# A decoder step on one core: the forget step on VectorE split, its subtraction six slots later; the memory's sums of squares three slots later

## The chip, the cores and the metric

The kernel runs on one core of one Trainium2 chip. The core's engines are TensorE (PE in the rows; its weight loads are PEld), VectorE (DVE), ScalarE (ACT), GpSimd (POOL) and SyncE (SP); 16 DMA engines move data between HBM and the on-chip memory. Each engine works through a queue of its own in order and meets the others at semaphores. The metric is the device time of one execution in microseconds (us).

## The reference, cut to what matters

One inference step of two layers, for a prompt of 256 positions and 8 samples of one position each: 264 columns in all. Layer 0 is a forgetting attention, layer 1 an RWKV-7 mixer. The change touches three things in layer 0: the log forget gates, the norm of the memory rows, and the order beside them.

```python
def rmsnorm(x, g):
    xf = x.astype(jnp.float32)
    y = xf * lax.rsqrt(jnp.mean(xf * xf, axis=-1, keepdims=True) + RMS_EPS)
    return (y * g.astype(jnp.float32)).astype(x.dtype)

def memory_kv(mem, g_mem, w_mem):
    b = mem.shape[0]
    k, v = jnp.split(rmsnorm(mem, g_mem) @ w_mem, 2, axis=-1)
...
def fox_layer(x, g_pre, g_post, w_in, b_f, w_o, mem_k, mem_v, attend):
    b, t, _ = x.shape
    h = rmsnorm(x, g_pre)
    q, k, v, f, q_mem, gate = jnp.split(h @ w_in, FOX_SPLITS, axis=-1)
...
    logf = jax.nn.log_sigmoid((f + b_f).astype(jnp.float32))
    o_tok = attend(q, k, v, logf)
    o_mem = memory_attend(q_mem, mem_k, mem_v)
    y = gated_output(o_tok, o_mem, gate, w_o)
    return x + rmsnorm(y, g_post), (k, v, logf)
```

A sample attends over 2048 past positions, 16 pages of 128 rows, 12 heads of 128: each page of keys or values is 128 x 1536 in float32, 768 KB.

## The kernel before, in words

**Slots.** The first part of the kernel (to some 790 us) is a loop of 155 slots, written out. A slot has three sorts of work. One key page of the samples (slots 0 to 135, 16 pages a sample) is multiplied with the sample's query on VectorE: 12 custom instructions of one head each, line 1920 (1897 for the first four pages). TensorE multiplies the value pages (line 1023, from slot 19 on) and does three small products a sample behind its last key page (`largest` L990 in slot 16, `spread_largest` L995 in slot 17, `denominators` L1000 in slot 19, for the first sample). And each slot has the steps of the prompt's side that `SLOT_STEPS` puts there. Every engine walks the same slots in the same order, and in each does its own part of them.

**What sets the order.** `STEPS0` is a list of steps, `COST` gives each a number, and `steps_of_slots` lays the list over the slots by the running sum of these numbers. A "unit" is a block of 256 output columns of the input projection: TensorE does it in four quarters (L733), and ScalarE copies each half out of PSUM (L1391).

**The forget step.** ("f", 0) on TensorE makes the gates' columns. ("f", 3), in slot 7, makes log sigmoid of them: VectorE adds the bias, takes the absolute value and the minimum with 0 (L1833 to L1836); ScalarE takes exp and log of it (L1483, L1485), each behind a load of its function table; VectorE waits for that (semaphore `f_act`) and subtracts (L1838), then spreads the samples' part over heads (L1840). ScalarE waits for the subtraction (`f_vec` at 2) and stores the result (L1487). ("f", 1), in slot 13, is a transpose on TensorE that waits for the same subtraction (L860), and a copy on ScalarE (L1490). ("lf", 1), in slot 8, is a scan and a subtraction on VectorE over the cached gates (L1853, L1854); ("lf", 2), in slot 14, six products of it on TensorE (L883, L884) and three copies on ScalarE (L1502), for which `largest` on VectorE waits (`lf_d`).

**The memory's norm.** ("ms", 0), in slot 20: ScalarE squares 16 rows of 256 columns (L1508). ("ms", 1): VectorE adds them in four instructions (L1858, L1859). ("ms", 2), slot 23: TensorE sums over the partitions (L888). ("ms", 3): VectorE makes the inverse root (L1801, L1803) with a root on ScalarE (L1398).

**The rings.** Key pages lie in a ring of four places, and value pages in another of four. GpSimd issues both sorts of loads in the order of the slots (L667): the key page of slot n waits until VectorE has used page n - 4 (`k_used`), the first four value pages go out in slots 13 to 16 behind the slots' key pages, later ones wait for TensorE (`v_used`). SyncE loads the weights, 2 MB a unit, and waits for TensorE to finish earlier units (`p_done`).

Of the kernel before, what the change touches and what calls it, by code (L numbers as in the profile page):

```python
# [18 lines left out]
T = NPR + NS  # L19
# [39 lines left out]
def shape_constants():  # L59
# [17 lines left out]
    for n in range(2):  # L77
# [9 lines left out]
UNITS += [("wm0", n, "m0", 2 * n) for n in range(4)]  # L87
FILL = [("wm1", n, "m1", 2 * n) for n in range(4)] + [("wg0", n, "g", 2 * n) for n in range(8)]
QROWS = 2
STEPS0 = [("f", 0), ("lf", 0), ("unit", 2), ("f", 3), ("lf", 1), ("unit", 3), ("f", 1), ("lf", 2), ("unit", 4), ("f", 2), ("ms", 0),  # L90
          ("ms", 1), ("unit", 5), ("ms", 2), ("ms", 3), ("unit", 6), ("mz", 0), ("mz", 1), ("unit", 7), ("mz", 2), ("mz", 3)]
STEPS0 += [("unit", 8 + n) for n in range(4)] + [("mr", 0, h) for h in range(MH)]
for n in range(FH // 2):
    for name, unit, kind in (("wkv", 2 * n, "k"), ("wkv", 2 * n + 1, "v")):
        STEPS0.append(("unit", len(UNITS)))
        UNITS.append((name, unit, kind, 2 * n))
        if n:
            STEPS0 += [("O", MH + 2 * n - 1)] if kind == "k" else []
        else:
            STEPS0 += [("S", 0), ("T", 0), ("S", 1), ("mn", 0), ("O", 0)] if kind == "k" else [("T", 1), ("mn", 1), ("S", 2), ("O", 1)]  # L100
    STEPS0.append(("vr", n))
    if n == 0:
        STEPS0 += [("T", 2), ("mn", 2), ("S", 3), ("O", 2), ("T", 3), ("mn", 3), ("dm", MH), ("O", 3)]
    a = MH + 2 * n
# [99 lines left out]

OV_COPIES, OV_TURNS = c_, len(V_ENDS)

COST = {"mn": 0.1, "mz": 0.1, "ms": 0.4, "lf": 4.0, "unit": 14.2, "S": 3.0, "T": 0.8, "O": 1.3, "vr": 0.8, "f": 3.0, "mr": 0.5, "self": 1.0, "gp": 0.3, "dm": 0.1}
TOTAL0 = sum(COST[x[0]] for x in STEPS0)
LAST_FILL = NK + 8


def steps_of_slots():
# [5 lines left out]
    for x in STEPS0:  # L218
        for part in [(*x, n) for n in range(4)] if x[0] == "unit" else [x]:
            out[min(sum(e <= spent / TOTAL0 + 1e-9 for e in ends), SLOTS - 1)].append(part)  # L220
            spent += COST[x[0]] / (4 if x[0] == "unit" else 1)
    return out
# [17 lines left out]
def trunk_step(nc, I, O):  # L240
    ctx = ExitStack()
    with ctx:
# [5 lines left out]
        def sem(name):  # L248
            if name not in sems:
                sems[name] = ctx.enter_context(nc.semaphore(name))  # L250
            return sems[name]
# [62 lines left out]
        S = r0.take(2, PAGES * FH)  # L314
# [1479 lines left out]
        def _(dve):  # L1794
# [4 lines left out]
            def inverse_root(o, n, buf):  # L1799
                dve.wait_ge(sem("n_ss"), o + 1)  # L1800
                ts(buf[:, 0:n], A[:, 0:n], 1.0 / D, RMS_EPS, ALU.mult, ALU.add).then_inc(sem("n_ms"), 1)  # L1801
                dve.wait_ge(sem("n_rt"), o + 1)
                ch.do(v_.reciprocal(buf[:, 0:n], buf[:, 0:n]))  # L1803

            def largest_score(o, causal, nm_):
                dve.wait_ge(sem("at_s"), o + 1)
                dve.wait_ge(sem("at_e"), o)
                if not causal:
                    for t in range(NT):
                        last = v_.tensor_reduce(nm_[:, t:t + 1], Xp[:, t * NPR:(t + 1) * NPR], AX.X, ALU.max, negate=True)  # L1810
                    last.then_inc(sem("at_m"), 1)
                    return

                for t in range(NT):
                    s = Xp[:, t * NPR:t * NPR + P * (t + 1)]
                    last = v_.tensor_tensor_reduce(s, s, mask3[:, t * P:t * P + P * (t + 1)], 1.0, -3e38,
                                                   ALU.add, ALU.max, mxk[:, t:t + 1])
                ch.do(last)
                ts(nm_, mxk, -1.0, None, ALU.mult).then_inc(sem("at_m"), 1)

            def weights(o, causal, Pw, rsum_, rinv_):
                dve.wait_ge(sem("at_e"), o + 1)
                ch.do(v_.reciprocal(rinv_, rsum_))
                for t in range(NT):
                    nk = P * (t + 1) if causal else NMEM
                    last = ts(Pw[:, t, 0:nk], Pw[:, t, 0:nk], rinv_[:, t:t + 1], None, ALU.mult)
                last.then_inc(sem("at_p"), 1)

            def step(name, *at):
                if name == "f" and at[0] == 3:  # L1830
                    dve.wait_ge(sem("vec_in2"), 64)
                    dve.wait_ge(sem("f_mm"), 1)
                    ch.do(ts(fpT, Y[0:FH, 0:T], bf[:, 0:1], None, ALU.add))  # L1833
                    ch.do(ts(ftmp, fpT, -1.0, None, ALU.mult))
                    tt(ftmp, ftmp, fpT, ALU.max).then_inc(sem("f_vec"), 1)
                    ch.do(ts(fpT, fpT, 0.0, None, ALU.min))  # L1836
                    dve.wait_ge(sem("f_act"), 2)
                    tt(fpT, fpT, ftmp, ALU.subtract).then_inc(sem("f_vec"), 1)  # L1838
                    dve.wait_ge(sem("f_vec"), 2)
                    tt(fd, ident[0:FH, 0:FH].unsqueeze(2).to_broadcast([FH, FH, NS]),  # L1840
                       fpT[:, NPR:T].unsqueeze(1).to_broadcast([FH, FH, NS]), ALU.mult).then_inc(sem("f_vec"), 1)
                elif name == "S":
                    largest_score(at[0], at[0] >= MH, nm)
                elif name == "T":
                    weights(at[0], at[0] >= MH, Pp, rsum, rinv)
                elif name == "dm":
                    dve.wait_ge(sem("const_in"), 16)
                    v_.memset(mask3[:, P:2 * P], 0.0)
                    v_.tensor_copy(mask3[:, 0:P], cst[:, C_CAUS:C_CAUS + P])
                    ch.do(v_.tensor_copy(mask3[:, 2 * P:], cst[:, C_CAUS:C_CAUS + P]))  # L1850
                elif name == "lf" and at[0] == 1:
                    dve.wait_ge(sem("lf_c"), 1)
                    ch.do(v_.tensor_tensor_scan(Fs, starts, lfT, 0.0, ALU.mult, ALU.add))  # L1853
                    tt(Fs, Fs, lfT, ALU.subtract).then_inc(sem("lf_fs"), 1)  # L1854
                elif name == "ms" and at[0] == 1:
                    dve.wait_ge(sem("n_sq"), 1)
                    for half in (8, 4, 2):
                        ch.do(tt(oT[:, 0:half, 0:NMEM], oT[:, 0:half, 0:NMEM], oT[:, half:2 * half, 0:NMEM], ALU.add))  # L1858
                    tt(oT[:, 0, 0:NMEM], oT[:, 0, 0:NMEM], oT[:, 1, 0:NMEM], ALU.add).then_inc(sem("n_sq"), 1)  # L1859
                elif name == "ms" and at[0] == 3:  # L1860
                    inverse_root(1, NMEM, rsm)
                elif name == "mz":
                    c = at[0]
                    for k in range(4 * c, 4 * c + 4):
                        last = stt(memv0[:, k, :], memv[:, k, :], gmem(0)[:, k:k + 1], rsm, ALU.mult, ALU.mult)
                    if c == 3:
                        last.then_inc(sem("n_out"), 1)
                elif name == "mn":
                    for k in range(4 * at[0], 4 * at[0] + 4):
                        last = stt(memv[:, k, :], memv[:, k, :], gmem(1)[:, k:k + 1], rsm, ALU.mult, ALU.mult)  # L1870
                    if at[0] == 3:
                        last.then_inc(sem("n_out"), 1)
                elif name == "self":
                    dve.wait_ge(sem("p_free"), M_OF["v", FH - 1] + 1 + 2)
                    dve.wait_ge(sem("f_vec"), 3)
                    dve.wait_ge(sem("mr_t"), 2 * MH)
                    dve.wait_ge(sem("stored_mem"), 64)
                    tt(prod, qT[:, 0:FH, NPR:T], kS, ALU.mult).then_inc(sem("self_p"), 1)
                    dve.wait_ge(sem("self_y"), 1)
                    v_.tensor_copy(selfS.rearrange("p h s -> p (h s)"), Y[:, 0:FH * NS])  # L1880
                    v_.tensor_copy(fS.rearrange("p h s -> p (h s)"), Y[:, FH * NS:2 * FH * NS]).then_inc(sem("self_out"), 1)
                elif name == "gp":
                    c = at[0]
                    dve.wait_ge(sem("p_free"), M_OF["g", 4 * c + 3] + 1 + 2)
                    dve.wait_ge(sem("at_o"), MH + FH)
                    tt(gT[:, 4 * c:4 * c + 4, 0:NPR], oT[:, 4 * c:4 * c + 4, 0:NPR], gT[:, 4 * c:4 * c + 4, 0:NPR],
                       ALU.mult).then_inc(sem("gp_out"), 1)
# [667 lines left out]
```

## Time and profile before

| what | us |
|---|---|
| median of 3 runs | 1744.52 |
| lowest and highest of them | 1740.86, 1747.26 |
| the profiled execution | 1743.76 |
| its span, first to last instruction | 1742.1 |
| TensorE busy in the span | 1622.8 |
| VectorE busy in the span | 1059.1 |

The span lies 1.7 us under the profiled execution's own time. Times in the rows below count from the span's start. A row of the timeline has start, duration, engine, line, operation, output and inputs, the number of instructions merged, and in brackets how long the engine stood idle ahead of it and who released it. The trace has two records for each float32 matmul of the program, so that a quarter of a unit, 8 matmuls, reads x16.

### The profile page before, as it was taken

What the parts mean: (1) busy time and instruction counts of PE and PEld (TensorE: products, weight loads), DVE (VectorE), ACT (ScalarE), POOL (GpSimd) and SP (SyncE); (2) the same over time, 40 slices, a digit from 0 to 9 for tenths busy, and PEclk for the clock granted to TensorE, in tenths of its full rate; (3) what the DMA queues carried; (4) which work ended last, traced back from release to release, by engine and by line L of the source; (5) the groups of instructions that cost most, each with busy time, mean ns of one, the idle gap of its engine ahead of it and who ended that gap; (6) DMA issues with size and microseconds to landing.
All of it is one profiled execution on the core that took longest, in us unless ns stands there. A gap on an engine that the chain in (4) does not pass through costs nothing.

```text
span 1742.1 us, 27840 instructions
## 1 busy us (share of the span) xinstructions
PE 1622.8 (93%) x9596; PEld 1290.3 (74%) x9596; DVE 1059.1 (61%) x4997; ACT 392.3 (23%) x978; POOL 160.8 (9%) x295
## 2 busy tenths in 40 slices
PE   7979999899999999988989999999999999999995
PEld 6657776677677777657977777777777777788895
DVE  4587555655465555437872467777777777340755
ACT  2112011201121111221120433333333333221011
POOL 1012111221111211220000000000000000020000
PEclk9989999999999999999989999999999999999998
DMA  9579999999999999995442233333332323374441
GB/s 384 206 284 373 420 417 397 379 396 420 405 400 422 418 420 412 357 372 234 146 189 96 102 102 103 101 101 101 101 100 101 102 76 115 108 271 170 145 146 51
DMA packets 101725, 419.95 MB, mean 241 GB/s; under 512 B 41796, under 2 KB 46288, under 8 KB 91984
## 3 DMA queue, kind: packets, MB, share of 16 engines
q0 software_dynamic: 41680, 218.91, 31.6%
q1 hardware_dynamic: 53256, 187.54, 28.4%
q10 hardware_dynamic: 6648, 11.73, 1.8%
q8 instruction: 76, 1.25, 0.3%
q14 instruction: 65, 0.53, 0.1%
HBM read 405.28 MB, written 12.85 MB: 240 GB/s over the span
## 4 chain that ended last, share of the span: by engine, by line
PE 75%; DVE 10%; DMA 6%; ACT 5%; issue 2%; SPq 0%; POOLq 0%; POOL 0%; ACTq 0%; DVEq 0%
PE psum L733 25%; PE psum L801 10%; PE psum L1160 10%; PE psum L783 6%; PE psum L1023 5%; DMA kvr<-in_cv 3%; PE psum L722 2%; PE psum L771 2%; PE psum L1207 2%; DMA kvr<-in_ck 1%; PE psum L1217 1%; PE psum L744 1%; PE psum L759 1%; PE psum L824 1%; ACT gT L1759 1%
## 5 line engine op out<-in xcount | busy, mean ns | idle before, releaser
L1920 DVE CUSTOM_DVE_ANT_0 kvr<-kvr,arena 128x128 f32<-128x128 f32 x1488 | 323.7, 287 | 115.3 <-DMA kvr<-in_ck 115.2
L733 PE MATMUL psum<-hT,wring 128*128 128x264 f32 x1536 | 367.9, 397 | 0.0
L733 PEld LDWEIGHTS psum<-hT,wring 128*128 128x128 f32 x1536 | 294.5, 195 | 67.9 <-issue 19.8
L1160 PE MATMUL psum<-hT,kvr 128*128 128x264 f32 x1152 | 283.3, 392 | 1.8 <-DVE hT L2248 1.8
L1160 PEld LDWEIGHTS psum<-hT,kvr 128*128 128x128 f32 x1152 | 214.0, 192 | 41.9 <-issue 8.9
L1920 DVE DVE_READ_ACCUMULATOR2_ANT arena<- 128x1 f32 x1488 | 122.4, 82 | 0.0
L783 PE MATMUL psum<-hT,kvr 128*128 128x264 f32 x512 | 120.2, 391 | 0.0
L783 PEld LDWEIGHTS psum<-hT,kvr 128*128 128x128 f32 x512 | 96.9, 193 | 16.2 <-issue 0.4
L667 POOL DMA_DIRECT2D kvr<-in_cv x128 | 67.7, 529 | 371.7 <-PE psum L1023 275.0
L1023 PE MATMUL psum<-kvr,arena 128*32 128x384 f32 x1024 | 97.1, 495 | 4.9 <-DMA kvr<-in_cv 4.9
L667 POOL DMA_DIRECT2D kvr<-in_ck x128 | 67.6, 528 | 235.0 <-issue 228.0
L801 PE MATMUL psum<-hT,wring 128*128 128x132 f32 x672 | 77.9, 277 | 0.0
L801 PEld LDWEIGHTS psum<-hT,wring 128*128 128x128 f32 x672 | 76.7, 191 | 0.0
L703 POOL DMA_DIRECT2D wring<-in_cmk x8 | 5.8, 722 | 744.8 <-PE psum L1306 744.8
L1023 PEld LDWEIGHTS psum<-kvr,arena 128*32 128x32 f32 x1024 | 27.0, 109 | 49.8 <-issue 41.2
L733 PE MATMUL psum<-oT,wring 128*128 128x256 f32 x256 | 57.7, 382 | 0.0
L733 PE MATMUL psum<-gT,wring 128*128 128x256 f32 x256 | 57.4, 382 | 0.0
L801 PE MATMUL psum<-gT,kvr 128*128 128x132 f32 x448 | 53.0, 277 | 2.3 <-DVE gT L2030 2.3
L733 PEld LDWEIGHTS psum<-gT,wring 128*128 128x128 f32 x256 | 48.0, 190 | 9.1 <-issue 3.1
L733 PEld LDWEIGHTS psum<-oT,wring 128*128 128x128 f32 x256 | 47.9, 191 | 9.1 <-issue 2.5
L801 PEld LDWEIGHTS psum<-gT,kvr 128*128 128x128 f32 x448 | 51.6, 191 | 3.0 <-DVE gT L2030 1.6
L2326 DVE TENSOR_TENSOR wring<-psum,wring 128x512 f32<-128x512 f32 x48 | 30.9, 686 | 33.2 <-PE psum L1207 32.1
(433 smaller groups left out, 2315.2 us busy)
## 6 DMA issues: line engine op xcount, KB each, us to landing
kvr<-in_ck POOLq DMA_DIRECT2D x128, 768.0 KB, 11.8
kvr<-in_cv POOLq DMA_DIRECT2D x128, 768.0 KB, 11.5
kvr<-in_wrkv SPq DMA_DIRECT2D x12, 3072.0 KB, 13.8
kvr<-in_wo SPq DMA_DIRECT2D x14, 2048.0 KB, 8.1
wring<-in_wkv SPq DMA_DIRECT2D x12, 2048.0 KB, 11.8
wring<-in_wm SPq DMA_DIRECT2D x8, 2048.0 KB, 11.9
wring<-in_wg SPq DMA_DIRECT2D x8, 2048.0 KB, 12.1
kvr<-in_wg SPq DMA_DIRECT2D x8, 2048.0 KB, 9.1
```

Of the source, the lines that this page charges most:

```text
L667: pool.dma_start(ring[:, n % KRING, :], I["c" + name][bass.ds(pid, 1)].rearrange("a p n -> (a p) n"))\
L722: last = mm(psum[:, bank, 0:n], w[:, k, t * P:(t + 1) * P], rhs[:, k, 0:n], start=(k == 0), stop=(k == KT - 1))
L733: last = mm(psum[:, m % 2, 0:n], w[:, k, t * P:(t + 1) * P], rhs[:, k, 0:n], start=(k == 0), stop=(k == KT - 1))
L744: last = mm(psum[:, t, 0:T], w[:, k, t * P:(t + 1) * P], hT[:, k, :], start=(k == 0), stop=(k == KT - 1))
L771: last = mm(psum[:, m % 2, 0:T], w[:, k, t % 2 * P:(t % 2 + 1) * P], hT[:, k, :], start=(k == 0), stop=(k == KT - 1))
L783: last = mm(psum[:, m % 2, 0:T], w[:, k, t * P:(t + 1) * P], hT[:, k, :], start=(k == 0), stop=(k == KT - 1))
L801: last = mm(few_bank(i, q), w[:, k, :], x[:, k, :], start=(k == 0), stop=(k == KT // 2 - 1))
L1023: last = mm(Vp[32 * c:32 * c + 32, 0:384], Ps[:, n % 2, j * FH:j * FH + 32], ring[:, v % VRING, c * 384:(c + 1) * 384], start=(j == 0), st ...
L1160: last = mm(psum[:, m % 2, 0:T], w[:, k, t * P:(t + 1) * P], hT[:, k, :], start=(k == 0), stop=(k == KT - 1))
L1207: last = mm((A, B)[h][:, n * 256:(n + 1) * 256], src[hp, c * P:(c + 1) * P], KR[hp, a, c, :], start=True, stop=True)
L1920: last = v_.tensor_tensor_reduce(page, page, qb[:, n % 2, h * P:(h + 1) * P], 1.0, 0.0, ALU.mult, ALU.add, S[:, n % 2, j * FH + h:j * FH + ...
L2326: tt(GM[:, a, q, :], (A, B)[q % 2], masks[:, K_RM:K_RM + 512], ALU.mult).then_inc(sem("gm_out"), 1)
```

## The change

The list of steps gets a new step ("fe", 0) of cost 0 in front of ("f", 1): VectorE's wait for `f_act`, the subtraction (L1838 before, L1839 now) and the spreading (L1840, L1841) go there, out of ("f", 3). ScalarE's part of ("f", 3) is not split: its wait for the subtraction and its store stay in slot 7. ("ms", 1) moves behind ("unit", 5). `TOTAL0` stays 601.9, so all other steps keep their slots, but for quarter 3 of unit 5, which comes from slot 23 into slot 22.

```diff
-STEPS0 = [("f", 0), ("lf", 0), ("unit", 2), ("f", 3), ("lf", 1), ("unit", 3), ("f", 1), ("lf", 2), ("unit", 4), ("f", 2), ("ms", 0),
-          ("ms", 1), ("unit", 5), ("ms", 2), ("ms", 3), ("unit", 6), ("mz", 0), ("mz", 1), ("unit", 7), ("mz", 2), ("mz", 3)]
+STEPS0 = [("f", 0), ("lf", 0), ("unit", 2), ("f", 3), ("lf", 1), ("unit", 3), ("fe", 0), ("f", 1), ("lf", 2), ("unit", 4), ("f", 2), ("ms", 0),
+          ("unit", 5), ("ms", 1), ("ms", 2), ("ms", 3), ("unit", 6), ("mz", 0), ("mz", 1), ("unit", 7), ("mz", 2), ("mz", 3)]
...
                     tt(ftmp, ftmp, fpT, ALU.max).then_inc(sem("f_vec"), 1)
                     ch.do(ts(fpT, fpT, 0.0, None, ALU.min))
+                elif name == "fe":
                     dve.wait_ge(sem("f_act"), 2)
                     tt(fpT, fpT, ftmp, ALU.subtract).then_inc(sem("f_vec"), 1)
```

The lines of VectorE's code move down by one. VectorE's queue in slots 7 and 8 before (`ftmp` and `fpT` lie in arena, a key page in kvr):

```order
L1834 TENSOR_SCALAR arena<-arena 12x264 [waits dve_step]
L1835 TENSOR_TENSOR arena<-arena 12x264 [waits dve_step]
L1836 TENSOR_SCALAR arena<-arena 12x264
L1838 TENSOR_TENSOR arena<-arena 12x264 [waits f_act,dve_step]
L1840 TENSOR_TENSOR arena<-cst,arena 12x96 [waits f_vec]
L1920 ISA kvr,arena<-kvr,arena 128x128 [waits k_full0]
```

The subtraction now stands behind key page 13, in slot 13 (the rows of the change; the first two end page 13, the last begins page 14):

```order
L1921 ISA kvr,arena<-kvr,arena 128x128
L1921 ISA arena 128x1
L1839 TENSOR_TENSOR arena<-arena 12x264 [waits f_act]
L1841 TENSOR_TENSOR arena<-cst,arena 12x96 [waits f_vec]
L1921 ISA kvr,arena<-kvr,arena 128x128 [waits k_full2]
```

So pages 8 to 13 and the scan of ("lf", 1) have come ahead of it. The memory's sums on VectorE, before, in slot 20, with page 21 behind them:

```order
L1858 TENSOR_TENSOR oT<-oT 128x8x256 [waits n_sq]
L1858 TENSOR_TENSOR oT<-oT 128x4x256 [waits dve_step]
L1858 TENSOR_TENSOR oT<-oT 128x2x256 [waits dve_step]
L1859 TENSOR_TENSOR oT<-oT 128x256 [waits dve_step]
L1920 ISA kvr,arena<-kvr,arena 128x128 [waits k_full1]
```

And now, in slot 23, with the inverse root and page 24 behind them:

```order
L1859 TENSOR_TENSOR oT<-oT 128x8x256 [waits n_sq]
L1859 TENSOR_TENSOR oT<-oT 128x4x256 [waits dve_step]
L1859 TENSOR_TENSOR oT<-oT 128x2x256 [waits dve_step]
L1860 TENSOR_TENSOR oT<-oT 128x256 [waits dve_step]
L1801 TENSOR_SCALAR arena<-psum 128x256 [waits n_ss]
L1803 RECIPROCAL arena<-arena 128x256 [waits n_rt]
L1921 ISA kvr,arena<-kvr,arena 128x128 [waits k_full0,dve_step]
```

Pages 21, 22 and 23 now stand ahead of the sums.

## Rows read from the trace of the kernel before

**Rows 1.** The page's first part: busy time of TensorE, share, instructions.

```profile
PE 1622.8 (93%) x9596; PEld 1290.3 (74%) x9596; DVE 1059.1 (61%) x4997; ACT 392.3 (23%) x978; POOL 160.8 (9%) x295
```

**Rows 2.** TensorE's waits, whole span: line, releaser, us in total, times, longest.

```profile
PE psum L990 <- DVE arena L1939: 11.7, 1, 11.7
...
PE psum L1023 <- DMA kvr<-in_cv: 4.9, 4, 2.0
```

**Rows 3.** Timeline of TensorE, slots 13 to 23.

```profile
100.95 0.29 PE L860 MATMUL psum<-cst,arena 12*128 12x12 f32 x2
...
106.42 3.72 PE L733 MATMUL psum<-hT,wring 128*128 128x264 f32 x16
121.84 0.38 PE L990 MATMUL psum<-cst,arena 128*12 128x128 f32 x1 [11.69 <-DVE arena L1939]
122.01 5.07 PE L733 MATMUL psum<-hT,wring 128*128 128x264 f32 x16
...
127.33 3.83 PE L733 MATMUL psum<-hT,wring 128*128 128x264 f32 x16
...
154.61 0.59 PE L888 MATMUL psum<-oT,cst 128*128 128x256 f32 x2
```

**Rows 4.** Timeline of VectorE, slots 7 to 15.

```profile
89.17 0.42 DVE L1838 TENSOR_TENSOR arena<-arena 12x264 f32<-12x264 f32 x1 [14.20 <-ACT arena L1485]
89.63 0.25 DVE L1840 TENSOR_TENSOR arena<-cst,arena 12x96 f32<-12x96 f32 x1
...
92.36 3.34 DVE L1853 TENSOR_TENSOR_SCAN oT<-kvr,oT 128x1536 f32<-128x1536 f32 x1
95.73 1.76 DVE L1854 TENSOR_TENSOR oT<-oT 128x1536 f32<-128x1536 f32 x1
...
110.70 0.29 DVE L1920 CUSTOM_DVE_ANT_0 kvr<-kvr,arena 128x128 f32<-128x128 f32 x1 [3.02 <-DMA kvr<-in_ck]
...
118.23 0.29 DVE L1920 CUSTOM_DVE_ANT_0 kvr<-kvr,arena 128x128 f32<-128x128 f32 x1 [1.12 <-DMA kvr<-in_ck]
...
121.30 0.48 DVE L1939 TENSOR_REDUCE arena<-arena 128x12 f32<-128x192 f32 x1
```

**Rows 5.** Timeline of ScalarE, slots 7 to 14.

```profile
85.62 1.28 ACT L1483 ACT_TABLE_LOAD   x1
...
90.25 0.60 ACT L1537 ACTIVATE arena<-psum 128x512 f32<-128x512 f32 x1 [1.18 <-DVE arena L1840]
...
106.63 1.09 ACT L1502 ACTIVATE arena<-psum 128x512 f32<-128x512 f32 x1 [0.63 <-PE psum L884]
```

**Rows 6.** Timeline of GpSimd: the issues of key pages 12, 13 and 15.

```profile
93.62 0.53 POOL L667 DMA_DIRECT2D kvr<-in_ck  x1 [18.30 <-issue]
101.23 0.53 POOL L667 DMA_DIRECT2D kvr<-in_ck  x1 [7.09 <-PE psum L733]
...
106.34 0.53 POOL L667 DMA_DIRECT2D kvr<-in_ck  x1 [0.88 <-issue]
```

**Rows 7.** Table by stretch: length, busy time of each engine, TensorE's clock, DMA share, GB/s.

```profile
80.00:100.00 20.00, 19.31 (x86) 15.60 (x85) 10.76 (x53) 5.98 (x9) 0.53 (x1) 1.00 0.12 41
110.00:122.00 12.00, 0.31 (x2) 0.16 (x2) 8.76 (x75) 0.00 (x0) 1.58 (x3) 0.69 1.02 422
...
155.00:200.00 45.00, 45.00 (x242) 34.57 (x242) 32.57 (x236) 4.44 (x9) 8.44 (x16) 1.00 1.01 418
```

**Rows 8.** Timeline of VectorE, slots 20 to 23.

```profile
140.77 4.28 DVE L1858 TENSOR_TENSOR oT<-oT 128x2048 f32<-128x2048 f32 x3 [3.92 <-ACT oT L1508]
145.08 0.42 DVE L1859 TENSOR_TENSOR oT<-oT 128x256 f32<-128x256 f32 x1
...
155.25 0.43 DVE L1801 TENSOR_SCALAR arena<-psum 128x256 f32<-128x256 f32 x1 [2.09 <-PE psum L888]
```

**Rows 9.** Timeline of TensorE, the same place for the second sample.

```profile
202.35 0.28 PE L990 MATMUL psum<-cst,arena 128*12 128x128 f32 x1
...
206.32 3.72 PE L733 MATMUL psum<-oT,wring 128*128 128x256 f32 x16
```

More of the change, by code:

```diff
@@ L205 @@
 OV_COPIES, OV_TURNS = c_, len(V_ENDS)
-COST = {"mn": 0.1, "mz": 0.1, "ms": 0.4, "lf": 4.0, "unit": 14.2, "S": 3.0, "T": 0.8, "O": 1.3, "vr": 0.8, "f": 3.0, "mr": 0.5, "self": 1.0, "gp": 0.3, "dm": 0.1}
+COST = {"mn": 0.1, "mz": 0.1, "ms": 0.4, "lf": 4.0, "unit": 14.2, "S": 3.0, "T": 0.8, "O": 1.3, "vr": 0.8, "f": 3.0, "mr": 0.5, "self": 1.0, "gp": 0.3, "dm": 0.1, "fe": 0.0}
 TOTAL0 = sum(COST[x[0]] for x in STEPS0)
```

## The prediction, made before the run

> **What bounds the kernel now.** I read the busy times first: TensorE works 1622.8 us of 1742.1, 93% [rows 1]. So what TensorE does without pause is the frame, and a change pays if it closes a gap of TensorE. The second view is TensorE's waits, longest first. In the slot part there is one large one: L990, `largest` of the first sample, waits once, 11.7 us, for VectorE's L1939 [rows 2]. The third view, TensorE's timeline, places it: a quarter of unit 4 ends at 106.42 + 3.72 = 110.14, and L990 starts at 121.84 [rows 3]. The fourth, VectorE's timeline, says why VectorE is late. At 89.17 - 14.20 = 74.97 it has done the first half of the forget step and then stands for 14.2 us until ScalarE's logarithm (L1485) is there [rows 4]. ScalarE is not slow, it is late: its first table load for this step starts at 85.62 [rows 5], since it walks the slots at TensorE's pace and copies units out before. VectorE was some 10 us ahead of the others and loses that lead to a wait that nobody needs so early: the one product that uses the subtraction, TensorE's L860, starts at 100.95, without a wait before it [rows 3].
>
> **The change: the subtraction, six slots later.** No instruction is added or taken away. The wait of 14.2 us in slot 7 goes, if the new place is behind 89.1, when the logarithm is done. What is late next? I walk VectorE forward from 74.97. A page takes 92.36 - 89.88 = 2.5 us, say 2.6 [rows 4]; the scan and subtraction of slot 8 take 3.34 + 1.76 = 5.1 us [rows 4].
> - Pages 8 to 11 were issued as pages 4 to 7 were done, all before 76. Between 80 and 100 the DMA engines moved 41 GB/s, 0.8 MB, which is page 12 alone [rows 6, 7]; so the four had landed by 80, page 8 first. I take it that none is waited for. So page 8 ends at 77.6, the scan at 82.7, page 9 at 85.3, page 10 at 87.9, page 11 at 90.5.
> - GpSimd issues page n + 4 some 1.2 us after page n is done: page 8 ended at 92.36, page 12 was issued at 93.62 [rows 4, 6]. So page 12 goes out at 78.9, 13 at 86.5, 14 at 89.1, 15 at 91.7. The value pages 0 to 3 go out between them.
> - Before, page 13 needed from 101.23 to 110.70, 9.5 us, and page 15 from 106.34 to 118.23, 11.9 us [rows 4, 6]. The DMA engines had that much room between 80 and 100 [rows 7] that the pages can come earlier. I take the long ones as the bound: page 13 at 96.0, 14 at 99.8, 15 at 103.6.
> - VectorE then ends page 13 at 98.6 at the latest (95.7 if the loads are quick), the subtraction at 99.1, page 14 at 102.4, page 15 at 106.2.
>
> **Who waits for the moved wait.** Three queues. TensorE's L860 needs the subtraction at 100.95: 1.9 us to spare in the slow case, 5 in the quick one. ScalarE's queue still has its wait for the subtraction in slot 7, and this is the side of the change that the list of steps does not show: ScalarE now stands from 89.1 to 96 or 99. Behind it stand the copy of the second sample's query (at 90.25 before [rows 5]), needed by VectorE's page 16 only, and the copies of unit 3 out of PSUM, needed by TensorE's unit 4 at 106.42 [rows 3]. It has 7 us for about 2 us of copies. The price is nothing, as long as VectorE reaches slot 13 before 101. The third queue is GpSimd's, which gains.
>
> **Then TensorE's gap.** `largest` on VectorE also waits for ScalarE's last copy of ("lf", 2), which ends at 106.63 + 1.09 = 107.72 [rows 5] and hangs on TensorE, not on VectorE. So L1939 ends at 107.7 and about 0.9 us for its two instructions (118.23 plus a page of 2.6 is 120.9, and L1939 ended at 121.78 [rows 4]): 108.6. TensorE comes to L990 at 110.14. The gap of 11.7 us is closed, with 1.5 us to spare. It had a tail: the granted clock over the gap was 0.69 [rows 7], and the first quarter of a unit after it took 5.07 us [rows 3], where a quarter takes 3.72. From L990 to the next quarter but one it was 127.33 - 121.84 = 5.49 us, and at the same place of the second sample 206.32 - 202.35 = 3.97 [rows 3, 9]. The whole term is (127.33 - 110.14) - 3.97 = 17.19 - 3.97 = **13.2 us**.
>
> The tail is what TensorE's clock does here: after 11.7 us without work it ran the first quarter in part at 1.2 of its 2.4 GHz. The Trainium skill (TensorE: Matmul & The Clock Gate, "What's actually happening") has it that the throttled clock is the default and activity releases it; by this rule the tail goes with the gap, and the trace agrees (5.07 against 3.72 us).
>
> **The change: the memory's sums, three slots later.** Before, VectorE waits 3.9 us in slot 20 for the squares, adds for 4.7 us, does three pages and then waits 2.1 us for TensorE's L888 [rows 8], which had started at 154.61 without a wait [rows 3]. VectorE is ahead at both ends, so the 3.9 us were not on the path, and taking them away is worth 0. The cost is a new danger: L888 now waits for sums that stand behind pages 21 to 23. Before, VectorE stood in slot 20 from 140.77 - 3.92 = 136.85 on; the sums took 4.7 us, the three pages 7.7 (145.50 to 155.25 - 2.09 = 153.16). Without loads in the way that is 149.3, 5.3 us before L888. With the loads at one page per 3.77 us (110.70 to 118.23 were two pages [rows 4]) it is 136.85 + 11.3 + 4.7 = 152.9, 1.7 us before. I take 0; between 0 and 3 us can be lost if a page comes late. All these times move with TensorE's 13 us, and VectorE's pages 16 to 19 will have been loaded while it waits. The quarter of unit 5 that goes from slot 23 into 22 only changes place with a copy of a query: 0.
>
> **What keeps the gain.** From 110 on every load is released by an engine, nothing by the clock on the wall. When TensorE comes to L990, at 110.1 instead of 121.8, the loads out (key pages up to 19, value pages to 3, the memory rows) are those that were out at 122 before. So the rest of the kernel should run as before, shifted by 13.2 us. Against the profiled execution of 1743.76 this gives 1730.6; its own time is 0.8 under the median of the three runs (1744.52), so I say **1730.8**. The sum's bounds: 11.7 if the clock's tail stays, and 13.2 + 2 if small waits that followed the gap go too.
>
> **Rivals.**
> 1. *The gain is given back to the loads.* From 155 to 200 the DMA engines moved 418 GB/s at a share of 1.01 while TensorE worked without a pause [rows 7], and TensorE waits for value pages four times, 4.9 us [rows 2]. If the stretch is as much bound by DMA as by TensorE, an earlier start only makes these waits longer. For it: the 5.1 MB that moved in the gap (422 GB/s for 12 us) were not idle time for DMA. Against it: the unused rate from 80 to 100 was (422 - 41) x 20 us = 7.6 MB, and the change pulls pages 12 to 16 and values 0 to 3, nine pages of 0.79 MB, 7 MB, forward to issues from 79 to 96. Half given back gives 1738, all of it 1744.
>    The Trainium skill (DMA: Bandwidth & Descriptors, "Issuing engines are not separate DMA queues") says that loads of all issuing engines run on the same 16 DMA engines and interleave. By it, key pages pulled forward stretch the weights and value pages beside them; what a row shows of it here is the range of 9.5 to 11.9 us for a page.
> 2. *The late subtraction.* If the loads do not come earlier, VectorE reaches slot 13 when it did before: page 13 from 110.70 to 113.3, the subtraction at 113.8. TensorE then stands at L860 from 100.95 for 12.8 us, with ScalarE stopped behind the same wait, and comes to L990 after another 9.2 us of work plus 1.3 for the clock, at 124.3 instead of 121.84: 2.5 us slower, 1747. With a page more of delay, or sums late at L888 by 3 us beside it, 1750 to 1754. It decides from the moment at which the subtraction is later than 101; every us beyond is one of TensorE. Against it stands the DMA engines' idle time from 80 to 100.
> 3. *The change does nothing*, if another wait holds VectorE in slots 8 to 12 for as long. I find none: the scan ran directly behind page 8 [rows 4], and GpSimd's issue at 93.62 had stood 18.3 us with nothing but VectorE's use of a page before it [rows 6]. 1743 to 1745.
>
> **How the numbers follow.** The forecast has 0.72, rival 1 0.18 (two thirds of it within 0.5%), rival 2 0.06 (half of it over 0.5% slower), rival 3 0.04. A measurement of this kernel tells about 0.5%, 8.7 us, from no change, so faster is below 1735.8. Faster: 0.72 + 0.06 = 0.78, less 0.02 for a forecast that falls short by 5 us: 0.76. Slower: 0.04, with the tail of rival 1. Same: 0.20. The range goes from 1727 (15 us and the scatter of the runs, which was 3 us to either side) to 1739, half of the gain given back.
>
> **What would show it.** In the profile of the changed kernel L1836 is followed by a page without a wait; L1839 has no wait before it and starts between 95 and 99; L860 is at 101 with no wait; L990 is at 110 with a wait under 1 us, and the quarter behind it takes 3.7 us. The granted clock there is 1.00. L888 stands 13 us earlier, at about 141, without a wait. From there to the end every stage keeps its length; rival 1 would show as more than 4.9 us of TensorE's waits for value pages, or for weights. The prediction is wrong if VectorE reaches slot 13 after 101, or if the stage from 155 to 790 us is longer than before.

## The result, and the profile after

The changed kernel takes 1732.7 us in the median of 9 runs (1727.6 to 1737.6), the kernel before, run beside it, 1740.9 (1737.6 to 1747.3). The ratio is 0.9945, 95% interval 0.9926 to 0.9965: 9.6 us, 6 to 13. Run once more on another chip (below) it gave 0.9923 (0.9900 to 0.9946). The forecast was 1730.8, from a gain of 13.2. The span of the profiled execution went from 1742.1 to 1734.0.

TensorE's timeline in slots 13 to 23, after (to be laid beside [rows 3]; columns as there):

```profile
101.21 0.29 PE L860 MATMUL psum<-cst,arena 12*128 12x12 f32 x2
...
106.68 3.72 PE L733 MATMUL psum<-hT,wring 128*128 128x264 f32 x16
110.24 0.27 PE L990 MATMUL psum<-cst,arena 128*12 128x128 f32 x1
110.35 3.73 PE L733 MATMUL psum<-hT,wring 128*128 128x264 f32 x16
114.01 0.39 PE L995 MATMUL psum<-arena,cst 12*128 12x12 f32 x2
114.32 3.83 PE L733 MATMUL psum<-hT,wring 128*128 128x264 f32 x16
120.02 0.39 PE L1000 MATMUL psum<-arena,cst 128*128 128x12 f32 x2 [1.87 <-DVE arena L1963]
120.26 5.50 PE L733 MATMUL psum<-hT,wring 128*128 128x264 f32 x16
...
144.58 0.60 PE L888 MATMUL psum<-oT,cst 128*128 128x256 f32 x2
```

L990 had waited 11.69 us and now stands directly behind its quarter; that quarter's successor takes 3.73 us where it took 5.07. Three slots on, the wait at L1000 for VectorE's sums of the first sample (L1963) has grown from 0.58 to 1.87 us, and the quarter behind it takes 5.50 us in place of 3.81, at a granted clock of 0.70. The same place before:

```profile
131.74 0.39 PE L1000 MATMUL psum<-arena,cst 128*128 128x12 f32 x2 [0.58 <-DVE arena L1962]
131.98 3.81 PE L733 MATMUL psum<-hT,wring 128*128 128x264 f32 x16
```

L888 comes at 144.58, where it had come at 154.61: 10.0 us earlier.

VectorE's timeline, slots 7 to 18, after (answers [rows 4]; the lines of its code are one higher):

```profile
75.72 0.28 DVE L1836 TENSOR_SCALAR arena<-arena 12x264 f32<-12x264 f32 x1
76.04 0.29 DVE L1921 CUSTOM_DVE_ANT_0 kvr<-kvr,arena 128x128 f32<-128x128 f32 x1
...
96.41 0.42 DVE L1839 TENSOR_TENSOR arena<-arena 12x264 f32<-12x264 f32 x1
97.49 0.29 DVE L1921 CUSTOM_DVE_ANT_0 kvr<-kvr,arena 128x128 f32<-128x128 f32 x1 [0.38 <-DMA kvr<-in_ck]
101.31 0.29 DVE L1921 CUSTOM_DVE_ANT_0 kvr<-kvr,arena 128x128 f32<-128x128 f32 x1 [1.19 <-DMA kvr<-in_ck]
108.06 0.36 DVE L1939 TENSOR_TENSOR arena<-arena 128x192 f32<-128x192 f32 x1 [4.11 <-ACT arena L1502]
108.46 0.49 DVE L1940 TENSOR_REDUCE arena<-arena 128x12 f32<-128x192 f32 x1
114.04 0.29 DVE L1921 CUSTOM_DVE_ANT_0 kvr<-kvr,arena 128x128 f32<-128x128 f32 x1 [2.09 <-DMA kvr<-in_ck]
119.48 0.48 DVE L1963 TENSOR_REDUCE arena<-arena 128x12 f32<-128x192 f32 x1
```

Behind L1836 a page follows at once. The subtraction (L1839) starts at 96.41 without a wait. VectorE waits at L1939 for ScalarE's copy, not for pages, and L1940 ends at 108.95, 1.3 us ahead of L990. The row that I had not foreseen is the one at 114.04: page 17, 2.09 us late. Its load was issued at 97.68, and the 2 MB of memory rows came in behind it:

```profile
97.68 0.53 POOL L667 DMA_DIRECT2D kvr<-in_ck  x1 [0.87 <-issue]
101.31 0.33 SPq L565 DMA_DIRECT2D gT<-in_memT  x1
```

ScalarE's queue shows the other side of the split; its timeline, slots 7 to 9, after (answers [rows 5]):

```profile
88.91 0.42 ACT L1485 ACTIVATE arena<-arena 12x264 f32<-12x264 f32 x1
96.86 0.58 ACTq L1487 DMA_DIRECT2D out_lf<-arena  x1
97.48 0.60 ACT L1537 ACTIVATE arena<-psum 128x512 f32<-128x512 f32 x1 [8.15 <-DVE arena L1841]
```

And by stretch (length, busy time of each engine, granted clock, DMA share, GB/s), after, beside [rows 7]:

```profile
80.00:97.00 17.00, 16.31 (x72) 12.94 (x71) 16.93 (x124) 5.00 (x7) 4.64 (x9) 1.00 0.61 207
97.00:110.00 13.00, 13.00 (x49) 8.74 (x48) 7.28 (x62) 4.61 (x7) 1.59 (x3) 1.00 1.03 430
```

The idle 20 us of the DMA engines (41 GB/s) have become 207 GB/s to 97, and from there to 110 they are full.

### The profile page after: what moved, and what is told of

Its sections match the earlier page's. It is cut to its first block, busy times and chain, and to the rows that moved or that the text cites. A ratio compares the mean times of both kernels' runs of the same rounds, so it can differ in the third digit from the quotient of the medians.

```text
span 1734.0 us, 27840 instructions
## 1 busy us (share of the span) xinstructions
PE 1627.5 (94%) x9596; PEld 1289.5 (74%) x9596; DVE 1058.9 (61%) x4997; ACT 392.2 (23%) x978; POOL 161.4 (9%) x295
## 4 chain that ended last, share of the span: by engine, by line
PE 76%; DVE 10%; ACT 5%; DMA 5%; issue 2%; POOLq 0%; POOL 0%; SPq 0%; ACTq 0%; DVEq 0%
PE psum L733 25%; PE psum L1160 10%; PE psum L801 10%; PE psum L783 6%; PE psum L1023 5%; DMA kvr<-in_cv 3%; PE psum L722 3%; PE psum L771 2%; PE psum L1207 2%; DMA kvr<-in_ck 1%; PE psum L1217 1%; PE psum L759 1%; PE psum L744 1%; ACT gT L1759 1%; PE psum L824 1%
## 6 DMA issues: line engine op xcount, KB each, us to landing
kvr<-in_ck POOLq DMA_DIRECT2D x128, 768.0 KB, 11.9
kvr<-in_wrkv SPq DMA_DIRECT2D x12, 3072.0 KB, 13.4
wring<-in_wkv SPq DMA_DIRECT2D x12, 2048.0 KB, 11.9
```

## The experiments

Each is timed against the kernel before on the same chip. Each is read at three places of its profile: L888 in slot 23, the first product of the next stage (L722, behind the 155 slots), and the end of the span. This table is collected from the timelines; a kernel with added lines has them one higher.

| run | wait at L990 | at L1000 | quarter behind L1000 | L888 | L722 | span | ratio, interval |
|---|---|---|---|---|---|---|---|
| before | 11.69 | 0.6 | 3.81 | 154.61 | 793.13 | 1742.1 | 1 |
| after | 0 | 1.87 | 5.50 | 144.58 | 780.21 | 1734.0 | 0.9945 (0.9926 to 0.9965) |
| e4, after again | 0 | 1.27 | 3.81 | 142.29 | 777.94 | 1731.5 | 0.9923 (0.9900 to 0.9946) |
| e1, split alone | 0 | 1.41 | 3.81 | 142.95 | 778.69 | 1728.3 | 0.9937 (0.9914 to 0.9960) |
| e2, sums alone | 12.32 | 0.57 | 3.81 | 155.42 | 791.52 | 1743.2 | 0.9992 (0.9977 to 1.0008) |
| e7, subtraction in slot 8 | 10.34 | 0 | 3.81 | 153.75 | 788.57 | 1739.6 | 0.9991 (0.9978 to 1.0004) |
| e11, in slot 9 | 0 | 3.72 | 6.25 | 147.71 | 783.44 | 1734.9 | 0.9953 (0.9937 to 0.9969) |
| e6, behind page 15 | 0 (L860: 1.56) | 0 | 3.81 | 142.76 | 774.19 | 1728.4 | 0.9950 (0.9935 to 0.9964) |
| e9, that and 8 us | 0 (L860: 10.28) | 0 | 3.81 | 154.16 | 787.94 | 1738.6 | 0.9988 (0.9976 to 1.0000) |
| e5, ScalarE's wait moved too | 0 | 1.58 | 3.81 | 143.15 | 775.04 | 1726.3 | 0.9924 (0.9895 to 0.9953) |
| e3, memory rows later | 0 | 0 | 3.81 | 141.19 | 775.38 | 1725.3 | 0.9922 (0.9902 to 0.9942) |
| e8, value pages later | 0 | 0.41 | 3.81 | 141.85 | 777.39 | 1727.2 | 0.9919 (0.9893 to 0.9946) |
| e10, slot 12, memory rows later | 0 | 0 | 3.81 | 141.72 | 777.61 | 1725.4 | 0.9901 (0.9885 to 0.9918) |

### Which part of the change it is: e1, e2, e4

e1 keeps the split and puts the sums back, e2 is the kernel before with the sums moved.

```diff
# e1, from the changed kernel
-          ("unit", 5), ("ms", 1), ("ms", 2), ("ms", 3), ("unit", 6), ("mz", 0), ("mz", 1), ("unit", 7), ("mz", 2), ("mz", 3)]
+          ("ms", 1), ("unit", 5), ("ms", 2), ("ms", 3), ("unit", 6), ("mz", 0), ("mz", 1), ("unit", 7), ("mz", 2), ("mz", 3)]
# e2, from the kernel before
-          ("ms", 1), ("unit", 5), ("ms", 2), ("ms", 3), ("unit", 6), ("mz", 0), ("mz", 1), ("unit", 7), ("mz", 2), ("mz", 3)]
+          ("unit", 5), ("ms", 1), ("ms", 2), ("ms", 3), ("unit", 6), ("mz", 0), ("mz", 1), ("unit", 7), ("mz", 2), ("mz", 3)]
```

> The subtraction in slot 13, the memory's sums back in slot 20. If the whole gain is the closed gap at L990, this keeps all of it: L990 at 110.2 without a wait, L888 at 144.6 as in the changed kernel (154.6 before), ratio to before 0.994 to 0.995. If the sums' move has a share, L888 comes later than 144.6 or the end lies up to 4 us (the wait of 3.9 us in slot 20) above the changed kernel's.

> The sums in slot 23, the forget step unsplit. By my working VectorE waits for TensorE at L888 either way, so nothing changes: L838 subtraction waits 14.2 us, L990 waits 11.7 us, L888 at 154.6, ratio 1.000 within 0.002. If the 3.9 us in slot 20 were on the path, L888 comes up to 3.9 us earlier; if the sums come late for L888 now, it waits and comes later.

> The changed kernel once more, on the same chip as the three others, as their reference. L990 at 110.2, L1000 waits about 1.9 us, L888 at 144.6; ratio to before 0.9945 (0.9926 to 0.9965). If the wait at L1000 or the half clock behind it differs between executions, it shows here.

The split alone gives the whole gain, ratio 0.9937; the sums alone nothing, 0.9992. VectorE's rows in slots 20 to 23 of e1 have the durations and waits of [rows 8] to a hundredth, 11.7 us earlier:

```profile
129.11 4.28 DVE L1859 TENSOR_TENSOR oT<-oT 128x2048 f32<-128x2048 f32 x3 [3.92 <-ACT oT L1508]
...
143.58 0.43 DVE L1801 TENSOR_SCALAR arena<-psum 128x256 f32<-128x256 f32 x1 [2.09 <-PE psum L888]
```

In the changed kernel the same VectorE waits nothing at the sums and 7.78 us at L1801 for TensorE: the wait has changed its place.

```profile
132.71 4.27 DVE L1859 TENSOR_TENSOR oT<-oT 128x2048 f32<-128x2048 f32 x3
...
145.21 0.43 DVE L1801 TENSOR_SCALAR arena<-psum 128x256 f32<-128x256 f32 x1 [7.78 <-PE psum L888]
```

e4 is the same program as the changed kernel and differs from its first profile by 2.3 us at L888:

```profile
119.42 0.39 PE L1000 MATMUL psum<-arena,cst 128*128 128x12 f32 x2 [1.27 <-DVE arena L1963]
119.66 3.81 PE L733 MATMUL psum<-hT,wring 128*128 128x264 f32 x16
```

0.60 us of these are the shorter wait, 5.50 - 3.81 = 1.69 the quarter behind it, which here ran at a granted clock of 1.00. So the wait at L1000 is the kernel's, the slow quarter is the execution's. e1, which has no slow quarter either, is to be laid beside e4 (142.95 and 142.29), not beside the 144.6 that I had expected from the first profile.

### What makes page 17 late: e3, e8

```diff
# e3
                 if u == 5:
                     sp.wait_ge(sem("p_done"), 8)
+                    sp.wait_ge(sem("d_t"), 3)
# e8
-V_EARLY = {VSLOT[0] - 2 * VRING + 2 + n: n for n in range(VRING)}
+V_EARLY = {VSLOT[0] - 2 * VRING + 4 + n: n for n in range(VRING)}
```

> The changed kernel, with the load of the memory rows (2 MB) issued behind the third product of lf 2, at 106.7 instead of 101.3. Theory A: key page 17 took 16.4 us (97.7 to 114.0) because this load shared the DMA engines with it. Then page 17 is there before VectorE wants it at 111.9, the wait of 1.9 us at L1000 goes, and with it the half clock of the quarter behind it (5.50 instead of 3.83 us): L888 at 144.6 - 1.9 - 1.7 = 141.0, ratio 0.992 to 0.993. Theory B: the value pages and key pages ahead of it make it late, and the memory rows do not matter: L1000 waits 1.9 us as before, L888 at 144.6. A third way: the rows then come late for the squares in slot 20, and L888 waits.

> The changed kernel, with the first four value pages issued two slots later (slots 15 to 18), so that they are not ahead of key pages 15 to 17 in GpSimd's queue; the memory rows as in the changed kernel. If key page 17 is late by the sum of what is in flight, and not by the memory rows in particular, this helps like the later memory rows did: L1000 without a wait or under 0.5 us, L888 at 141 to 142. If it is the memory rows alone, the 1.3 to 1.9 us at L1000 stay. Value page 0 is needed at 126; two slots later it is still there.

Both mend it. With the memory rows issued at 107.4 instead of 101.3, page 17 is used at 112.3 without a wait, and TensorE has no idle time at all from 97 to 142 (PE busy 45.00 of 45.00; the two rows are e3 and the changed kernel):

```profile
97.00:142.00 45.00, 45.00 (x219) 33.88 (x218) 32.21 (x251) 13.17 (x20) 7.92 (x15) 1.00 0.98 392
```

```profile
97.00:142.00 45.00, 43.13 (x200) 31.67 (x199) 32.49 (x253) 12.18 (x18) 7.95 (x15) 0.96 0.96 379
```

TensorE's row at L1000 (one line higher in e3) stands without a wait, and the quarter behind it is a fast one:

```profile
118.42 0.29 PE L1001 MATMUL psum<-arena,cst 128*128 128x12 f32 x2
118.56 3.81 PE L734 MATMUL psum<-hT,wring 128*128 128x264 f32 x16
```

With the value pages two slots later page 17 is in time too (used at 112.3), but page 18 is 0.6 us late, and L1000 waits 0.41. So theory A of e3, the memory rows in particular, is too narrow: page 17 is late by the sum of what is in flight with it. e3 brings 2 MB in 6.1 us later. The edit of e8 does less than its expectation says: value pages 0 and 1 still go out ahead of page 17 (93.65, 96.19 and 97.61), only value pages 2 and 3 (98.96 and 101.92), 1.5 MB, go out behind it, and that does the same. L888 comes at 141.19 and 141.85, where I had expected 141.0 and 141 to 142.

### The place of the subtraction: e7, e11, e6, e9, e5

```diff
# e7 (here and in e11 the part of the list that differs)
- ("f", 3), ("lf", 1), ("unit", 3), ("fe", 0), ("f", 1)
+ ("f", 3), ("fe", 0), ("lf", 1), ("unit", 3), ("f", 1)
# e11
+ ("f", 3), ("lf", 1), ("fe", 0), ("unit", 3), ("f", 1)
# e6: no "fe" in the list; in VectorE's loop
                 if slot < NK:
                     page_scores(slot)
+                if slot == 15:
+                    step("fe", 0)
# e9: as e6, and ahead of the step
+                    dve.wait_ge(sem("f_act"), 2)
+                    for _ in range(24):
+                        ch.do(ts(ftmp, ftmp, 1.0, None, ALU.mult))
# e5: ScalarE
                     ac(ftmp, ftmp, ACT.Ln, bias=1.0).then_inc(sem("f_act"), 1)
+                elif name == "fe":
                     act.wait_ge(sem("f_vec"), 2)
                     act.dma_start(O["lf"], fpT).then_inc(sem("stored_lf"), 16)
```

> The changed kernel, with the subtraction in slot 8, behind page 8 and ahead of the scan. VectorE then waits from 78.6 to 89.2, 10.6 of the 14.2 us. If it is the wait's length that makes the gap at L990, through key pages that are issued late, L990 waits 11.7 less one page of 2.6 us, about 9 us, the clock's tail stays, and L888 is at 152: ratio 0.998. If any place behind the first key page did, the gap would be closed as in the changed kernel.

> The changed kernel, with the subtraction behind page 9 and the scan. VectorE is there at 86.3 and waits 3 us instead of 14.2. A middle dose for the way from VectorE's wait to TensorE's gap (0 us: no gap; 10.7 us: 10.3; 14.2 us: 11.7). Pages 14 and 15 go out some 3.5 us later than in the changed kernel, so page 15 is used from about 107.5, L1939 ends at 111 to 112, L990 waits 0.5 to 2 us. If the gap goes with the wait's length one to one, without a part that VectorE's slack hides, L990 waits 2.5 us or more.

The early side. With a wait of 10.69 us left on VectorE, L990 still waits 10.34. I had expected about 9: the pages' loads lost more than the one page brought. Page 13 was issued at 99.0, where it had been 101.2, and was in time; page 14, issued at 101.6, was 5.5 us late, at 113.5.

```profile
120.91 0.38 PE L990 MATMUL psum<-cst,arena 128*12 128x128 f32 x1 [10.34 <-DVE arena L1940]
121.09 5.98 PE L733 MATMUL psum<-hT,wring 128*128 128x264 f32 x16
```

With a wait of 3.81 us (e11) the gap at L990 is gone, but it has not vanished: it stands at the third product of the sample, L1000:

```profile
110.56 0.27 PE L990 MATMUL psum<-cst,arena 128*12 128x128 f32 x1
...
122.19 0.60 PE L1000 MATMUL psum<-arena,cst 128*128 128x12 f32 x2 [3.72 <-DVE arena L1963]
122.64 6.25 PE L733 MATMUL psum<-hT,wring 128*128 128x264 f32 x16
```

This missed my expectation (0.5 to 2 us, at L990). Pages 16 and 17 were 1.4 and 2.5 us late for VectorE. L888 is at 147.71, 6.9 us before that of the kernel before, where the changed kernel had 10.0 and 12.3. From a wait of 3.81 us to one of 10.69 TensorE's gap grew from 3.72 to 10.34 us, about one for one. By time alone e11 (0.9953) is not told from the changed kernel's first measurement (0.9945).

> The changed kernel, with the subtraction on VectorE two pages later, behind page 15, at about 104.0. Rival 2's rule, every us behind 101 is one of TensorE: L860 starts at 104.5 with a wait of 3.3 us, and all behind it shifts: L990 at 113.5, L888 at 145.6 to 148 (3.3 us behind the changed kernel's 142.3 to 144.6). If ScalarE's queue, released that late, adds a wait of its own, or the clock falls at L860, it is 1 to 3 us more. Ratio 0.994 to 0.997.

> As the run with the subtraction behind page 15, with 24 small VectorE instructions (a multiplication by 1 of a 12 x 264 tile) ahead of it, about 8 us: the subtraction ends at about 111 instead of 103. A dose of rival 2: every us beyond 101 is one of TensorE, less the 1.3 to 1.9 us that the wait at L1000 can absorb. L860 waits 9 to 10 us, the clock's tail is back (1.3 to 2.2 us), L990 at about 121, L888 at 151 to 153 (before 154.6, the changed kernel 142.3 to 144.6). Ratio 0.998 to 1.000. If VectorE's lead in pages made up for a stop of TensorE, L888 would come earlier than 149.

The late side.

```profile
103.21 0.29 PE L860 MATMUL psum<-cst,arena 12*128 12x12 f32 x2 [1.56 <-DVE arena L1839]
```

In e6 the subtraction starts at 102.74, L860 waits 1.56 us, and L990 is at 112.24, 2.0 us behind the changed kernel's. So far rival 2's rule holds. But then page 17 is no longer late for TensorE, L1000 does not wait, and L888 comes at 142.76, between the two profiles of the changed kernel. The expectation of 3.3 us more at L888 was wrong: a wait of 1.6 us at L860 took the place of one of 1.3 to 1.9 at L1000. In e9 nothing absorbs it:

```profile
111.45 0.38 PE L860 MATMUL psum<-cst,arena 12*128 12x12 f32 x2 [10.28 <-DVE arena L1839]
111.77 2.08 PE L883 MATMUL psum<-oT,cst 128*128 128x512 f32 x2
...
120.09 3.72 PE L733 MATMUL psum<-hT,wring 128*128 128x264 f32 x16
```

L860 waits 10.28 us, and the products behind it take up to 2.08 us where they take 1.1 at the full clock; L888 is at 154.16, 0.5 us before that of the kernel before, ratio 0.9988. I had expected L888 at 151 to 153; it came 1.2 us later than that. Rival 2 was priced about right: a subtraction 10 us too late costs the whole gain; the clock's tail is dearer there, 120.09 - 111.45 = 8.6 us for what takes 5.5 (101.21 to 106.68 in the changed kernel), 3.2 where the prediction had put 1.3.

> The changed kernel, with ScalarE's wait for the subtraction and its store moved into the new step too (slot 13), so that ScalarE no longer stands from 89 to 97. My reason says that nobody needs its copies in that time: L860 at 101.2, L990 at 110.2, L888 at 142 to 145 as in the two profiles of the changed kernel, ratio 0.992 to 0.9945. If the standing queue had a price (the query's copy or unit 3's copies late), L888 comes 1 to 3 us earlier than 142.

ScalarE no longer stands from 89 to 97: it copies the query at 89.8 and half a unit at 94.7. L990 has no wait and L1000 one of 1.58 us, L888 is at 143.15, inside the two profiles of the changed kernel. That ScalarE stands for 8 us in slot 7 costs nothing here.

### The two mends together: e10

```diff
# VectorE's loop, no "fe" in the list; and the wait for d_t of e3
+                if slot == 12:
+                    step("fe", 0)
                 if slot < NK:
                     page_scores(slot)
```

> The changed kernel with the two mends together: the subtraction ahead of page 12 (at 91, behind the logarithm at 89.3, so that no engine waits for it) and the load of the memory rows behind lf 2. No wait of TensorE from 86 to 141: L990 at 110.3 and L1000 at 118.2 without waits, L888 at 141.2 to 141.6. Against the changed kernel's runs (0.9945 and 0.9923) 0.991 to 0.993: 1.3 us less is hardly to be told by time, the profile tells it.

1726.4 us in the median (1725.0 to 1727.1), ratio 0.9901 (0.9885 to 0.9918): the fastest of all. Its interval does not meet that of the changed kernel's first measurement (0.9926 to 0.9965), but it does meet the second's (0.9900 to 0.9946), and the three were not timed side by side. Nothing in its profile up to L888 is better than in e3, which has the later memory rows alone (141.72 against 141.19), and slot 12 was not run without them, so what the earlier subtraction adds is not shown. What the profile shows is no wait at L991 and L1001, and that the sums in slot 23 are now just late:

```profile
141.72 0.70 PE L889 MATMUL psum<-oT,cst 128*128 128x256 f32 x2 [0.15 <-DVE oT L1861]
```

Page 23 came 5.64 us late for VectorE there, and the sums behind it ended at 141.66. The place that the second half of the change gives to the sums costs nothing in the changed kernel and has no reserve left in this one; in e8 the sums ended at 141.45, 0.4 us before L888.

## Why the prediction was right, and where it was off

- **What bounds: right.** Without a gap at L990 the kernel is faster, and e2, e7 and e9, in which TensorE still stands for 10 to 12 us at L990 or L860, are within 0.12% of the kernel before.
- **The walk of VectorE: right, to a microsecond.** I had page 13's end at 95.7 to 98.6 (it was 96.5), L1939's end at 108.6 (L1940 ended at 108.95), L990 at 110.1 (110.24).
- **Who waits for the moved wait: right.** L860 did not wait, ScalarE stood from 89.3 to 97 and nobody missed it; e5 shows this by itself.
- **The term of 13.2 us: its first part right, its end too early.** The gap and the clock's tail at L990 are gone: from the end of the quarter before it to the start of the next quarter but one it is 114.32 - 110.40 = 3.92 us, where it was 17.19; I had 3.97. But I ended the sum there. The step that failed is the sentence that pages 16 to 19 "will have been loaded while it waits". Page 16 was; page 17, issued at 97.68, was there at 114.04, 16.4 us. My bound of 9.5 to 11.9 came from the first and the fifth page of the burst of eight that went out between 101.2 and 110.0 before, beside the memory rows; page 16, the seventh of it, already took 13.1, in rows that I had not taken:

```profile
108.88 0.53 POOL L667 DMA_DIRECT2D kvr<-in_ck  x1 [0.86 <-issue]
...
122.00 0.29 DVE L1920 CUSTOM_DVE_ANT_0 kvr<-kvr,arena 128x128 f32<-128x128 f32 x1 [0.21 <-DMA kvr<-in_ck]
```

  The same slip is in "What keeps the gain": at 110 the loads that are out are those of 122 before, as I said, but issued is not landed. Now five key and four value pages go out between 87.5 and 97.7, page 17 is the last of the nine, and the memory rows come in at 101.3 while it is in flight; the DMA engines were full from 97 on (430 GB/s, above). That made the wait of 1.9 us at L1000 (1.3 more than before) and in this execution 1.7 us of slower clock: 13.2 - 1.3 - 1.7 = 10.2, and L888 came 10.0 earlier; TensorE was at L860 0.3 us later than before (101.21, 100.95), which is the rest. In e4, without the slow quarter, it was 12.3; in e3, with the loads in another order, 13.4. TensorE comes to L860 up to 0.9 us later than before in the runs that do not wait there; counted from L860 the gains are 10.3, 12.6 and 14.1. The last is more than 13.2 because the wait of 0.6 us at L1000 went too, which I had put only into the sum's upper bound.
- **The number 1730.8: in part luck.** The gain was 8.2 us by the medians, 5.0 under the 13.2. But I had counted from the median of three runs, 1744.52, and over nine runs the kernel before has 1740.86, 3.7 us less. And my last step was a slip: 1730.6 and the 0.8 us give 1731.3, not 1730.8. So 1730.8 lies only 1.9 us under the measured time (5.0 - 3.7 + 0.5) because two errors go opposite ways.
- **The clock.** The tail at L990 went with the gap, as the rule cited from the Trainium skill (TensorE: Matmul & The Clock Gate, "What's actually happening") has it. That an idle time of only 1.9 us can be followed by a quarter of 5.5 us I had not reckoned with: the granted clock was 1.00 while TensorE stood (118.0 to 120.1) and 0.70 in the quarter behind (120.2 to 125.8); e4, e1 and e5 had 1.3, 1.4 and 1.6 us there and no slow quarter, e11 3.7 us and one of 6.25. Nor is the tail behind a long gap a fixed sum: after 10.34 us the first quarter took 5.98 us (e7), after 11.69 and 12.32 us 5.07 and 5.08 (before, e2).
- **The memory's sums: right.** Worth 0 (e2), at no cost (e1 against e4); the reserve before L888, which I had at 1.7 to 5.3 us, was 144.58 - 137.43 = 7.2 in the changed kernel and 142.29 - 139.27 = 3.0 in e4.
- **What keeps the gain: right behind L888; rival 1 true only for what stands ahead of it.** The part of the 13.2 us that was not won went to a late load with the DMA engines full, which is rival 1's mechanism, but at one key page and for 3.0 us at most. The stretch that rival 1 named did not get longer. From L888 to L722 it was 793.13 - 154.61 = 638.5 us before and 780.21 - 144.58 = 635.6 after, and between 631.4 and 636.1 in all the others. TensorE's waits for value pages are what they were (answers [rows 2]; in_cv, after):

```profile
PE psum L1023 <- DMA kvr<-in_cv: 4.8, 4, 1.9
```

  Over the whole stretch TensorE stood idle for 30.3 us before and 30.3 after, and for 29.6 to 31.0 in all thirteen profiles, so its waits took nothing back.

- **From profile to median.** The stage behind L722 has the same program in all of these kernels and took 1742.1 - 793.13 = 949.0 us before and 953.8 after, and between 947.8 and 954.2 in the others. This scatter of 6.4 us is as large as half of the forecast gain, and it is not in the waits: TensorE stands 61.7 to 62.9 us of the stretch in all thirteen profiles, and its busy time for the same records goes from 885.5 to 891.9. The two rows are before and after (TensorE's busy time is the second number):

```profile
793.00:1740.00 947.00, 886.81 (x5439) 740.77 (x5439) 614.01 (x1516) 250.18 (x628) 11.54 (x16) 0.98 0.35 125
780.00:1730.00 950.00, 891.66 (x5439) 742.84 (x5439) 613.20 (x1516) 250.18 (x628) 11.56 (x16) 0.98 0.35 124
```

  By the profiles alone the gain is 8.1 us, 10.0 + 2.9 - 4.8; by the medians 8.2; by the ratio 9.6. The forecast of 13.2 lies just outside the interval of the first measurement (6 to 13) and inside that of the second (9 to 17).

Open is what made the stretch from L888 to L722 2.4 to 7.1 us shorter in all twelve other profiles than in the one of before, the kernel with the moved sums alone included (636.1). It is TensorE's busy time again, 608.3 us before and 601.6 to 605.7 in the others, not its waits. One profile of each kernel does not tell this from the scatter of the stage behind it.

## What to carry to other kernels

An engine that runs ahead may lose its lead to a result that it needs only much later. Look for the consumer of the waiting instruction: if it starts long after the wait ends, the wait is in the wrong place, and moving it costs no work. When a stall of a consumer of a ring goes, its loads come in one burst: take the latency of the last of the burst, not of the first, and look at the first few users behind the old gap, since the gap may be found again there, smaller. A list of slots may have more than one place that works: here slot 13 was good, slot 12 too (run only with the later memory rows), 15 cost a wait of 1.6 us at L860 and took one away at L1000, and slots 8 and 9 were not good. Where a forecast comes out near the measured time, compare the gain and the time it was counted from one by one: here their errors went opposite ways.

## What the runs showed of the hardware that was not expected

- One key page of 768 KB, issued by GpSimd, took 9.5 us as the first, 11.9 as the fifth and 13.1 as the seventh of a burst of eight pages beside a 2 MB load, and 16.4 us as the last of nine that were issued within 10.2 us (each counted from its issue to VectorE's first use of it, for which VectorE waited), with the 2 MB load coming in behind them, at 422 to 430 GB/s.
- After an idle time of TensorE of 1.87 us a stretch of 16 recorded matmuls took 5.50 us instead of 3.81; after 1.27, 1.41 and 1.58 us, in three other profiles at the same place, it took 3.81. After 10.28 us the products took up to 2.08 us instead of 1.1, and the loss was 3.2 us. With quarters of a unit behind the gap the loss was 2.3 us after 10.34 us, and 1.3 after 11.69 and 12.32.
- The same 950 us of program, in thirteen profiles, differed by 6.4 us; all of it was TensorE's busy time (885.5 to 891.9 us), while its idle time stayed within 61.7 to 62.9 us.
